# The second mixer's compression, query transposes and compressed scores, moved into half steps of its projection

## What is computed

```python
def nsa_pool_mixer(x, w_in, cmp_pos, cmp_w1, cmp_b1, cmp_w2, pool_w, pool_scale, w_out):
    h = x @ w_in                                  # 1024 -> 512 q, 768 k/v, 24 gates, 512 u
    ...
    kc = compress_blocks(k_cmp, cmp_pos[0], cmp_w1[0], cmp_b1[0], cmp_w2[0])   # gelu(flat @ w1 + b1) @ w2
    vc = compress_blocks(v_cmp, cmp_pos[1], cmp_w1[1], cmp_b1[1], cmp_w2[1])   # 15 blocks of 32 positions
    ...
        s_c = jnp.einsum('bghqd,bgcd->bghqc', qb, kc)       # the compressed scores
        p_c = masked_softmax(s_c, cmp_end[None, :] <= t[:, None])
        o_c = jnp.einsum('bghqc,bgcd->bghqd', p_c.astype(vc.dtype), vc)
        ...                                       # o_s over selected blocks, o_w over a window, softmax each
        o = gb[..., 0:1] * o_c + gb[..., 1:2] * o_s + gb[..., 2:3] * o_w
    o_pool = pool_mixer(u, pool_w, pool_scale)
    return jnp.concatenate([o_nsa, o_pool], axis=-1) @ w_out
```

## Time and profile before

| | |
|---|---|
| median of 3 runs | 1038.02 us (1036.09 to 1038.51) |
| the profiled execution | 1040.25 us, its span 1038.4 us |
| mean granted TensorE clock | 0.981 |
| TensorE, weight loads | 975.5 us (94%), 821.2 us (79%) |
| VectorE, ScalarE, GpSimd | 659.3 us (63%), 469.8 us (45%), 52.9 us (5%) |
| read from memory | 185.13 MB, 179 GB/s over the span |

### The profile page before, as it was taken

The page is one execution under the profiler, slowest core; times in us unless marked ns, Lnnn a source line. Parts: engine busy times, 40 slices in busy tenths (PEclk is TensorE's granted clock), DMA queues, the critical chain, the costliest instruction groups (busy, mean ns, idle before and its releaser), DMA issues.

```text
span 1038.4 us, 14788 instructions
## 1 busy us (share of the span) xinstructions
PE 975.5 (94%) x5566; PEld 821.2 (79%) x5566; DVE 659.3 (63%) x820; ACT 469.8 (45%) x700; POOL 52.9 (5%) x58
## 2 busy tenths in 40 slices
PE   4888989899999999999979999998999989999996
PEld 1566877689999987976679999996786779999995
DVE  4757798885554575555776554557554786555555
ACT  2255555554544544424425544542554725444440
POOL 2031110100000001000020000000000010000000
PEclk9999999999999999879999999999999999999998
DMA  9959867858466576411347466453553357556531
GB/s 288 305 131 299 220 184 243 294 171 277 163 195 207 165 254 158 132 44 58 102 134 260 162 198 207 162 195 130 161 154 112 97 174 259 181 176 202 189 121 41
DMA packets 105624, 186.93 MB, mean 180 GB/s; under 512 B 8433, under 2 KB 58625, under 8 KB 105553
## 3 DMA queue, kind: packets, MB, share of 16 engines
q1 hardware_dynamic: 100160, 176.28, 52.8%
q0 software_dynamic: 2592, 8.53, 2.9%
q10 hardware_dynamic: 2818, 1.40, 0.5%
HBM read 185.13 MB, written 1.05 MB: 179 GB/s over the span
## 4 chain that ended last, share of the span: by engine, by line
PE 76%; DVE 10%; issue 4%; ACT 4%; DMA 2%; POOL 2%; POOLq 0%; ACTq 0%; DVEq 0%
PE PJ L1723 13%; PE PJ L1724 13%; PE PJ L1725 13%; PE AT L1865 8%; PE AT L1864 8%; PE AT L1863 8%; PE AT L1946 2%; DVE wlo L1041 2%; POOL rstd L444 2%; DVE acc L1062 1%; ACT whi L557 1%; PE AT L1714 1%; DMA raw<-in_w_out_dram 1%; DMA raw<-in_w_ada_dram 1%; DVE bn L1123 1%
## 5 line engine op out<-in xcount | busy, mean ns | idle before, releaser
L1863 PE MATMUL AT<-hT_hi,whi 128*128 128x256 f32 x720 | 203.8, 283 | 0.0
L1865 PE MATMUL AT<-hT_hi,wlo 128*128 128x256 f32 x720 | 203.7, 283 | 0.0
L1864 PE MATMUL AT<-hT_lo,whi 128*128 128x256 f32 x720 | 203.7, 283 | 0.0
L1041 DVE TENSOR_TENSOR wlo<-raw,whi 128x1024 fp32r<-128x1024 f32 x144 | 172.6, 1222 | 47.8 <-ACT whi L557 46.9
L1166 DVE TENSOR_TENSOR wlo<-raw,whi 128x1024 fp32r<-128x1024 f32 x144 | 169.8, 1222 | 32.0 <-ACT whi L615 31.2
L1723 PE MATMUL PJ<-whi,uhi 128*128 128x512 f32 x432 | 170.9, 396 | 1.5 <-DVE wlo L1041 0.9
L557 ACT ACTIVATE whi<-raw 128x1024 fp32r<-128x1024 f32 x144 | 146.3, 1054 | 55.4 <-DMA raw<-in_w_in_dram 35.8
L1724 PE MATMUL PJ<-wlo,uhi 128*128 128x512 f32 x432 | 169.3, 392 | 0.0
L1725 PE MATMUL PJ<-whi,ulo 128*128 128x512 f32 x432 | 168.7, 391 | 0.0
L615 ACT ACTIVATE whi<-raw 128x1024 fp32r<-128x1024 f32 x144 | 144.3, 1049 | 47.4 <-PE PJ L1725 43.9
L1723 PE MATMUL PJ<-whi,hT_hi 128*128 128x512 f32 (+1 forms) x336 | 139.5, 415 | 11.5 <-DVE hT_lo L1080 3.9
(11 more groups left out here) (291 smaller groups left out, 1043.4 us busy)
## 6 DMA issues: line engine op xcount, KB each, us to landing
raw<-in_mlp_w_dram SPq DMA_DIRECT2D x128, 512.0 KB, 4.7
raw<-in_w_ada_dram SPq DMA_DIRECT2D x48, 512.0 KB, 6.2
raw<-in_w_in_dram SPq DMA_DIRECT2D x32, 512.0 KB, 6.5
raw<-in_w_mlp_in_dram SPq DMA_DIRECT2D x32, 512.0 KB, 4.9
raw<-in_w_mlp_out_dram SPq DMA_DIRECT2D x32, 512.0 KB, 5.0
raw<-in_c_w_in_dram SPq DMA_DIRECT2D x24, 512.0 KB, 4.5
raw<-in_a_w_in_dram SPq DMA_DIRECT2D x12, 512.0 KB, 4.9
raw<-in_w_out_dram SPq DMA_DIRECT2D x8, 512.0 KB, 5.4
```

Of the source, the lines that this page charges most:

```text
L1041: tt(wlo[:, n % SPL, :], raw_slot(r), whi[:, n % SPL, :].bitcast(F32), ALU.subtract).then_inc(raw_done, 1)
L1863: mm(o, whi[:, s % SPL, c], hT_hi[:, k, :], start=first, stop=False, skip_group_check=True)
L1864: mm(o, whi[:, s % SPL, c], hT_lo[:, k, :], start=False, stop=False, skip_group_check=True)
L1865: ins = mm(o, wlo[:, s % SPL, c], hT_hi[:, k, :], start=False, stop=last, skip_group_check=True)
```

## The change

Small work is now called within a tile too: `tile_of` takes a list `middle` that it runs between its two halves, and `mixer` looks for it under the key (k, "within"). `compress` and `cmp_scores` are called once for each of their two parts. Behind tile 7, one part of the compression moves into the tile; of the four query transposes one moves into tile 8 and one into tile 9; the first part of the compressed scores moves into tile 10, ahead of `S_(6)`, and the second from behind tile 10 into tile 11. VectorE's `cmp_max` goes from step 10 to 11, `cmp_probs` from 11 to 12, and ScalarE does `cmp_exp` before `exps(7)` in place of after.

```diff
-                11: [lambda: block_out(B_AIN + 2, T_AIN + 12, 1024, 280), branch_gates, lambda: exps(7), cmp_exp],
+                11: [lambda: block_out(B_AIN + 2, T_AIN + 12, 1024, 280), branch_gates, cmp_exp, lambda: exps(7)],
...
-                10: [lambda: maxima(6), cmp_max],
-                11: [gates_out, lambda: weigh(6), lambda: maxima(7), cmp_probs],
-                12: [lambda: maxima(8), lambda: probs_out(6), lambda: weigh(7)],
+                10: [lambda: maxima(6)],
+                11: [cmp_max, gates_out, lambda: weigh(6), lambda: maxima(7)],
+                12: [cmp_probs, lambda: maxima(8), lambda: probs_out(6), lambda: weigh(7)],
...
-            def tile_of(pb, s0, i, n=512):
+            def tile_of(pb, s0, i, n=512, middle=()):
...
                     if i == 0:
                         bank_wait(pb, t)
+                    if t == 1:
+                        for step in middle:
+                            step()
...
-                            tile_of(pb + b, s0 + BLK * b, i, n)
+                            tile_of(pb + b, s0 + BLK * b, i, n, between.get((BLK * b + i, "within"), ()))
...
-            def compress():
+            def compress(i):
...
-            def cmp_scores():
+            def cmp_scores(t):
...
-                7: [compress], 8: [lambda: nsa_transposes(3), lambda: nsa_transposes(4)],
-                9: [lambda: nsa_transposes(5), lambda: nsa_transposes(6), compress2],
-                10: [lambda: S_(6), cmp_scores],
-                11: [lambda: S_(7)],
+                (7, "within"): [lambda: compress(0)], 7: [lambda: compress(1)],
+                (8, "within"): [lambda: nsa_transposes(3)], 8: [lambda: nsa_transposes(4)],
+                (9, "within"): [lambda: nsa_transposes(5)], 9: [lambda: nsa_transposes(6), compress2],
+                (10, "within"): [lambda: cmp_scores(0)], 10: [lambda: S_(6)],
+                (11, "within"): [lambda: cmp_scores(1)], 11: [lambda: S_(7)],
```

More of the change, by code:

```diff
@@ L2222, in nsa_transposes @@
                 ins.then_inc(nt_tr, 1)
-            def compress():
[L2226 to L2231, removed]
+            def compress(i):
+                pe.wait_ge(kb_done, i + 1)
+                for m in range(16):
+                    ins = mm(AT[0:64, 0, 32 * i:32 * i + 30], acc[:, 1024 * i + 64 * m:1024 * i + 64 * (m + 1)],
+                             acc[:, KB + 480 * i + 30 * m:KB + 480 * i + 30 * (m + 1)], start=m == 0, stop=m == 15)
+                if i == 1:
+                    ins.then_inc(c_mm, 1)
             def compress2():
@@ L2237, in compress2 @@
                     .then_inc(c2_mm, 1)
-            def cmp_scores():
+            def cmp_scores(t):
                 pe.wait_ge(c2_done, 2)
                 pe.wait_ge(nt_done, 7)
[L2242 to L2247, removed]
+                for h in range(8):
+                    ins = mm(AT[:, 0, 256 + HC * t + NCMP * h:256 + HC * t + NCMP * (h + 1)],
+                             qT[0:64, h * S + t * P:h * S + (t + 1) * P],
+                             gel[:, 0, NCMP * (h // 4):NCMP * (h // 4 + 1)], start=True, stop=True)
+                if t == 1:
+                    ins.then_inc(cs_mm, 1)
             def cmp_transposes():
```

## The result

The change made the kernel slower: 1041.69 us, the median of seven runs (1040.47 to 1042.09), against 1038.02 us (1036.09 to 1041.06) for the kernel before beside it. The ratio is 1.0032, with a 95% interval of 1.0019 to 1.0045. The profiled execution took 1042.09 us, its span 1040.3, the mean granted clock 0.977, in place of 0.981.

A forecast was written before the change was run, and what follows sets the result against it. TensorE was taken as the bound, at half clock in the edited stretch. The terms -7.3 + 0.95 + 0.1 + 0.3 = -5.95 us from the profiled 1040.25 gave 1034.3 us; the 8-in-10 range was 1032.0 to 1040.5.

The forecast's parts named there:

- What bounds the kernel: Whole kernel: TensorE, busy 94% of the span, sets the time; the edited stretch is compute at half clock, not weight waits.
- Part 1: Compressed scores, tile 11, group 7's scores and tile 12: half clock costs 7.3 us, all on the path.
- I take it that the clock mostly holds: Tiles 10 to 12 after the edit: the new mixture mostly keeps full clock, gaining 7.3 us; clock kept, costs as summed: 0.50.
- the fall comes and lasts longer: Rival, around tiles 10 to 12: the mixture cannot bring the clock back; 1043.4 us as profiled, 1041.2 beside the median; chance 0.13.
- The rule of the Trainium skill: Edited stretch: the edit removes no gap, so clock unchanged and only costs added; same time as the same-fall rival, 1039.4 us, 0.15.
- Part 2: Tiles 7 to 11, each interrupted once more: five switches at some 0.19 us cost 0.95 us, bounds 0.45 and 2.
- Part 3: Compressed scores' first half, within tile 10: TensorE waits 0.1 us for VectorE's second write, bounds 0 and 0.7.
- Part 4: VectorE and ScalarE order: group 8's scores wait 0.3 us longer for group 7's exponentials, bounds 0 and 1.5.
- The sum's base: Whole kernel: the summed -5.95 us was taken from the profiled execution's 1040.25 us, giving 1034.3; against the median, -3.7 us.

The follow-up runs named there:

- the run with wide passes: The change plus six useless full-height passes of 512 columns behind each half of the compressed scores: 1034.53 us, ratio 0.9981 to the kernel before.
- the compressed scores alone: The change with tiles 7 to 9 put back as in the kernel before, keeping the split compressed scores and helpers' order: 1039.17 us, ratio 1.0027.
- the two variants that left TensorE's compressed scores in one piece: Against the kernel before: only the change's spreading over tiles 7 to 9, 1037.29 us; only its helpers' order, 1038.26 us.
- the thin ballast: The change plus twelve useless passes of 64 rows and 15 columns behind each half of the compressed scores: 1044.43 us, ratio 1.0081 to the kernel before.
- the first wide-tile version: The kernel before with the compressed scores' halves moved within 512-column tiles 12 and 13, dependent work one to three steps later: 1041.09 us, ratio 1.0042.
- the second, without the wait: Compressed scores within tiles 12 and 13, with VectorE's compressed probabilities moved to step 13 and their transposes later in step 14: 1034.56 us, ratio 0.9981.

## Why the prediction was wrong, point by point

**What bounds the kernel: right.** TensorE's stream with its granted clock set the time, and the helpers never did in this stretch.

**Part 1, the price of the stretch: right.** 7.3 us of half clock, from pairs in one trace, against 22.16 - 14.8 = 7.4 from the run with wide passes. But none of it was gained, since the next step failed.

**"I take it that the clock mostly holds": the step that failed.** I compared the new mixture with two stretches that kept 1.00, whole 512-column tiles among attention work and the 30-column compression, and set aside that its half tiles are narrow. Those two weren't near enough. The 280-column half tile is six passes in 0.8 us, and between 1.9 us of 15-column passes and 2.3 us of 64-row scores it didn't keep the clock in any of these profiles: the clock fell in group 6 in the change's first and with the compressed scores alone, and already in tile 10's second half in the change's other one. The term of -7.3 us was nothing: 22.23 us from tile 10 to group 6's transposes, against 22.16 before. The pair of wide and thin ballast shows that the thinness of the mixture is the cause. The rival "the fall comes and lasts longer" is what happened, with its mechanism (once at 0.50 the mixture doesn't bring the clock back, tile 12 does) and nearly its number: 1041.2 forecast, 1041.69 measured. Its stretches were 17 to 20 us, against 17 and 14 in the kernel before, and 10 in the two variants that left TensorE's compressed scores in one piece. What the prediction overlooked is that the edit also takes tile 11 apart. Of the four profiles with tile 11 whole, two have the clock back right behind it, in group 7; of the four that split it without wide ballast (the change twice, the compressed scores alone, the thin ballast), none has it back before tile 12 is half done. The rival's nearness in number is in part luck: its switches and stall were 0.7 us too dear, and in the first profile the clock fell later than it supposed. I gave it 0.13. The reasoning for it stood in the text, and the stretch of the first trace, where tile 11 between two thin pieces had not brought the clock back, spoke for it more than the two others spoke against.

The rule of the Trainium skill that I weighed there (page "TensorE: Matmul & The Clock Gate", section "Why this matters for your kernels"), idle gaps as what costs throughput in mid-kernel, would have left the clock as it was. Its outcome was nearer than mine, but not its reason: the runs with ballast differ by 10 us without any gap. A gap seems to matter as well: in the profile of the first wide-tile version the clock fell behind the 3.13 us wait, and in that of the second, without the wait, it stayed at 1.00 there.

**Part 2, the switches: right in kind, too dear.** From the start of tile 7 to that of tile 10, three more switches cost 0.37 us, 0.12 each for my 0.19 (12.25 us before, 12.62 after, by the two starts in either timeline):

```profile
418.13 0.39 PE L1723 MATMUL PJ<-whi,hT_hi 128*128 128x512 f32 x1
```

That is the start before, and 430.38 its end; after, it is this row and the 432.17 above:

```profile
419.55 0.39 PE L1723 MATMUL PJ<-whi,hT_hi 128*128 128x512 f32 x1
```

Five make 0.6 us. The median of the runs with these three alone is within 0.1 us of the kernel before.

**Part 3, the earlier compressed scores: right.** VectorE's timeline of the kernel after, answering:

```profile
432.38 0.67 DVE L1486 TENSOR_TENSOR proj<-AT,cst 120x512 f32<-120x512 f32 x1
444.22 0.41 DVE L1507 TENSOR_TENSOR proj<-AT,cst 128x240 f32<-128x240 f32 x1 [0.59 <-PE AT L2246]
449.70 0.69 DVE L1288 TENSOR_REDUCE nmax<-AT 128x4 f32<-128x512 f32 x1 [0.76 <-PE AT L1950]
```

The second write ends at 433.05 and the first compressed pass starts at 433.13: a wait of 0.1 to 0.2 us, as forecast.

**Part 4, the helpers' order: the stall of 0.3 us wasn't put to the test.** In the change, at half clock, tile 12 covers everything. Where the stretch ran at full clock, with wide ballast, TensorE came to group 8's scores at 451.06, behind the transposes that began at 450.53, with no wait. But there it had 1.5 us of ballast between groups 6 and 7, and the helpers' chain doesn't move with that. From 440.31, where group 6's scores give way to tile 11, the chain runs on with no wait that the ballast causes: VectorE comes to group 7's maxima at 448.57, 0.7 us after the scores have ended, and ScalarE's last exponential ends at 450.7. That is 10.4 us. These are the rows for the ballast, the maxima and that exponential:

```profile
443.17 1.66 PE L2255 MATMUL AT<-whi,hT_hi 128*128 128x512 f32 x6
448.57 0.68 DVE L1288 TENSOR_REDUCE nmax<-AT 128x4 f32<-128x512 f32 x1
450.33 0.37 ACT L747 ACTIVATE pr<-AT,nmax 128x128 f32<-128x128 f32 x1
```

TensorE takes 451.06 - 440.31 = 10.75 us for its side, 9.25 without the ballast (the prediction had 10.1 for the chain and 9.7 for TensorE). So with the clock kept and no ballast, group 8's scores would wait about 1.1 us. That is an estimate from these rows; it lies within the forecast's bounds of 0 and 1.5, and above its 0.3.

**The sum's base: mis-sized too.** I subtracted the whole 7.3 us from the profiled 1040.25 without knowing how long the stretch is in a typical execution. Against medians, a kept clock with five switches would have given less than the 3.7 us forecast if the stretch is 10 to 14 us in the median execution; how long it is there wasn't measured, since the timed runs have only a mean clock.

**What the loss is made of.** By the line through the 104 executions, the change's first seven lie 1.2 us above the kernel before at equal mean clock, and the ten later ones also 1.2 us. Of this the switches are 0.6, by Part 2. The remaining 2.5 us or so go with the lower mean clock (medians 0.977 and 0.980, against 0.982). The last 0.6 us are not accounted for; the half-clock stretch falls on other work than before, but that is an argument, not a measurement.

## What to carry to other kernels

Before small matmuls are spread between others to hold TensorE's clock, look at what they are spread between: narrow half tiles around thin passes lost the clock for longer than the compact order (17 to 20 us against 10 to 17), while the same passes within 512-column tiles measured 0.2% below the kernel before, at the edge of the noise. Splitting a tile for it also takes away the whole tile behind which the clock may come back. Test the cause with ballast: a few useless wide passes that make a kernel faster, next to thin ones that don't, show in two runs what a trace leaves open. And when an execution's time hangs on the clock's falls, compare the profiled execution with the mean clocks of many others before pricing anything from it.

## What the runs showed of the hardware that was not expected

- TensorE's granted clock fell from 1.00 to 0.50 with the engine busy for all of the 3.9 us before, in windows of the profile, and stayed there 17 to 20 us while half tiles of 280 columns alternated with thinner passes.
- Twelve extra passes of 512 columns made the change 6 to 7 us faster (1034.53 against 1041.69 and 1040.52); passes of 64 rows and 15 columns in their place made it 3 to 4 us slower (1044.43).
- Once at 0.50, the clock came back within group 7's scores in two of four profiles in which tile 11, 280 columns wide, ran whole (10 us at half clock), and in none of four in which thin passes split it (17 to 20 us).
- One and the same program spreads over 9.6 us on one chip (1032.65 to 1042.21 in 47 executions of the kernel before), in step with its mean clock (0.67 us for 0.001, from 104 executions on four chips).
